# Regrouping TensorE's work in two attentions: two score steps together, values between two transpositions

## What is computed

```python
# "second attention" of the kernel: chunk_attention, 8 heads of 64, relative bias
s = einsum('bqhd,bkhd->bhqk', qch, kb) * scale + bias
p = softmax(where(valid, s, NEG_INF));   out = einsum('bhqk,bkhd->bqhd', p, vb)
# "third attention": mla_attention, 8 heads, q and k of 96 (64 + 32 rotated), v of 64
s = einsum('bqhd,bkhd->bhqk', qi, k) * scale
p = softmax(where(mask, s, NEG_INF));    out = einsum('bhqk,bkhd->bqhd', p, v)
```

## Time and profile before

| | |
|---|---|
| runs | 1180.93, 1180.98, 1180.99 us (median 1180.98) |
| profiled execution, its span | 1179.3 us |
| TensorE busy | 1169.2 us (99%) |
| VectorE, ScalarE, POOL busy | 571.2, 516.3, 455.4 us |
| second attention, first scores to last values | 661.3 to 706.5 us |
| third attention, first scores to last values | 726.2 to 775.1 us |

### The profile page before, as it was taken

One profiled execution on the slowest core, in us unless ns is written; L12 is line 12 of the kernel. 1 busy time (PEld: TensorE's weight loads), 2 busy tenths in 40 slices (PEclk: granted clock), 3 DMA queues, 4 the chain that ended last, 5 costly groups with the idle time before them and its releaser, 6 DMA issues.

```text
span 1179.3 us, 16136 instructions
## 1 busy us (share of the span) xinstructions
PE 1169.2 (99%) x5968; PEld 961.5 (82%) x5968; DVE 571.2 (48%) x1128; ACT 516.3 (44%) x816; POOL 455.4 (39%) x181
## 2 busy tenths in 40 slices
PE   9999999999999999999999999999999999999998
PEld 7887778988888888888988677789888888888887
DVE  4375245877777774212574567726434334340000
ACT  5444663634434442322546576835543443431110
POOL 6451224344344434444443211034434434434442
PEclk9999999999999999999999999999999999999999
DMA  8233122545544542223332110122322232212322
GB/s 310 81 108 107 37 76 104 205 176 190 213 184 174 211 156 83 98 98 109 127 137 91 54 37 1 37 72 73 107 108 94 84 107 107 75 70 98 98 98 96
DMA packets 27570, 132.39 MB, mean 112 GB/s; under 512 B 3456, under 2 KB 4608, under 8 KB 18688
## 3 DMA queue, kind: packets, MB, share of 16 engines
q1 hardware_dynamic: 25632, 129.23, 30.9%
q10 hardware_dynamic: 1888, 2.49, 0.7%
HBM read 129.61 MB, written 2.10 MB: 112 GB/s over the span
## 4 chain that ended last, share of the span: by engine, by line
PE 97%; ACT 2%; issue 0%; POOL 0%; DMA 0%; DVE 0%; DVEq 0%; ACTq 0%
PE psum L1544 87%; PE psum L1613 2%; PE psum L1625 2%; PE psum L2054 1%; PE psum L1774 1%; ACT prob L705 1%; PE psum L1867 1%; PE psum L1990 1%; ACT probT L688 1%; PE psum L1968 0%; POOL wl L488 0%; DMA gains_and_h<-x_first 0%; PE psum L1832 0%; PE psum L1998 0%; PE psum L1583 0%
## 5 line engine op out<-in xcount | busy, mean ns | idle before, releaser
L472 POOL TENSOR_TENSOR wl<-raw,wh 128x2048 fp32r<-128x2048 f32 (+2 forms) x89 | 365.6, 4108 | 495.1 <-ACT wh L621 285.3
L1544 PE MATMUL psum<-xh,wh 128*128 128x512 f32 (+1 forms) x1016 | 386.0, 380 | 1.2 <-POOL wl L488 1.1
L1544 PE MATMUL psum<-xl,wh 128*128 128x512 f32 (+1 forms) x1016 | 381.7, 376 | 0.0
L1544 PE MATMUL psum<-xh,wl 128*128 128x512 f32 (+1 forms) x1016 | 381.7, 376 | 0.0
L1190 DVE SCALAR_TENSOR_TENSOR scratch<-psum,cols,scratch 128x511 f32<-128x511 f32 (+1 forms) x176 | 131.7, 748 | 195.4 <-ACT scratch L766 186.4
L1544 PEld LDWEIGHTS psum<-xh,wh 128*128 128x128 f32 x1016 | 191.0, 188 | 40.6 <-issue 3.1
L1544 PEld LDWEIGHTS psum<-xh,wl 128*128 128x128 f32 x1016 | 191.1, 188 | 34.9
L1544 PEld LDWEIGHTS psum<-xl,wh 128*128 128x128 f32 x1016 | 191.2, 188 | 34.4 <-issue 0.2
L621 ACT ACTIVATE wh<-raw 128x2048 fp32r<-128x2048 f32 (+1 forms) x50 | 88.4, 1767 | 244.9 <-PE psum L1544 244.9
L1544 PE MATMUL psum<-acth,wh 128*128 128x512 f32 (+1 forms) x374 | 141.0, 377 | 0.0
L1544 PE MATMUL psum<-actl,wh 128*128 128x512 f32 (+1 forms) x374 | 140.8, 377 | 0.0
(11 more groups left out here) (264 smaller groups left out, 1383.1 us busy)
## 6 DMA issues: line engine op xcount, KB each, us to landing
raw<-stream SPq DMA_DIRECT2D x69, 1024.0 KB, 4.7
ada_raw<-ada SPq DMA_DIRECT2D x48, 512.0 KB, 5.4
raw<-down SPq DMA_DIRECT2D x32, 704.0 KB, 4.0
outT<-gains_and_h SPq DMA_DIRECT2D x8, 256.0 KB, 5.3
gains_and_h<-xT SPq DMA_DIRECT2D x7, 256.0 KB, 5.9
raw<-stream SPq DMA_DIRECT2D x7, 256.0 KB, 6.3
rel<-rel_tiles ACTq DMA_DIRECT2D x1, 1344.0 KB, 9.2
raw<-stream SPq DMA_DIRECT2D x2, 512.0 KB, 3.9
```

The costliest lines, as they stand in the source:

```text
L472: pool.tensor_tensor(wl[slot][:, 0:w], raw[slot][:, 0:w], wh[slot][:, 0:w].bitcast(F32), ALU.subtract).then_inc(lo_done, 1)
L1544: ins = pe.matmul(out, lhs[a], rhs[b], start=first and n == 0, stop=last and n == 2)
```

## The change

In the second and third attention TensorE's loop goes over pairs of steps, `u`: the scores of steps 2u and 2u+1, the transposition of step 2u-3, the values of steps 2u-5 and 2u-4, and the transposition of step 2u-2. Other work of the two steps (`beside`) stands behind both scores, but for u = 0. ScalarE keeps copy ahead of exponentials in even steps and takes the exponentials first in odd ones. The heads' high and low parts are taken one step later. The first attention keeps its order; its code is only moved into functions.

```diff
+        def values_of_pair(u):
+            last = STEPS // 2 + LAG // 2 - 1
+            return [x for x in (2 * u - 5, 2 * u - 4) if 0 <= x < STEPS] + ([STEPS - 1] if u == last else [])
+
+        def heads_step(a, p):
+            return TB * (p + 1) + LAG + (a > 0)
...
                 for step in range(STEPS + LAG):
-                    if TURN_LAG <= step < STEPS + TURN_LAG:
+                    turn = TURN_LAG <= step < STEPS + TURN_LAG
+                    behind = a > 0 and step % 2 == 1
+                    if turn and not behind:
                         turned(step)
...
+                    if turn and behind:
+                        turned(step)
                     if beside is not None:
                         beside(step)
-                    if step > TB + LAG - 1 and (step - LAG) % TB == 0:
-                        heads_high(a, (step - LAG) // TB - 1)
+                    for p in range(PAIRS - 1):
+                        if step == heads_step(a, p):
+                            heads_high(a, p)
...
+            def attend_by_two(a, ready, scores, v, prob, probT, ident, beside):
+                for u in range((STEPS + LAG) // 2):
+                    for step in (2 * u, 2 * u + 1):
+                        if step < STEPS:
+                            step_scores(a, step, ready, scores, None)
+                        if u == 0:
+                            beside(step)
+                    for step in (2 * u, 2 * u + 1):
+                        if u > 0:
+                            beside(step)
+                    if 0 <= 2 * u - TURN_LAG < STEPS:
+                        step_turned(a, 2 * u - TURN_LAG, prob, ident)
+                    for x in values_of_pair(u):
+                        step_values(a, x, v, probT)
+                    if 0 <= 2 * u + 1 - TURN_LAG < STEPS:
+                        step_turned(a, 2 * u + 1 - TURN_LAG, prob, ident)
...
-            attend(1, chunked_ready, chunked, None, v2, prob2, probT2, ident2, last_values_and_first_heads)
+            attend_by_two(1, chunked_ready, chunked, v2, prob2, probT2, ident2, last_values_and_first_heads)
...
-            attend(2, latent_ready, latent, None, v3, prob2, probT2, ident2, last_heads)
+            attend_by_two(2, latent_ready, latent, v3, prob2, probT2, ident2, last_heads)
```

More of the change, by code:

```diff
@@ L1257, in attend @@
                         dve.tensor_scalar(prob[V % 4][:, 1, 0:w], prob[V % 4][:, 1, 0:w], row_sum[:, c + 1:c + 2], None, ALU.mult).then_inc(att.norm, 1)
-                    if step > TB + LAG and (step - LAG - 1) % TB == 0:
-                        heads_low(a, (step - LAG - 1) // TB - 1)
+                    for p in range(PAIRS - 1):
+                        if step == heads_step(a, p) + 1:
+                            heads_low(a, p)
                     if after is not None and step >= STEPS:
@@ L1583, in norm_sum, with step_scores, step_turned, step_values @@
                 pe.matmul(SS_BANKS[j][:, half(j)], ones[:, :], ss_acc[:, half(j)], start=True, stop=True).then_inc(norm.ss, 1)
+            def step_scores(a, step, ready, scores, decays):
+                V, p, i, w = unit(a, step), step // TB, step % TB, width(step)
+                outs = scores_banks(a, V)
+                ready(step)
+                if a == 0 and step:
+                    pe.wait_ge(att.max, 2 * V - 1)
+                elif a == 1 and step >= 2:
+                    pe.wait_ge(att.max, 2 * V - 2)
+                elif step >= 2:
+                    pe.wait_ge(att.raw, 2 * step - 2)
+                for e in range(2):
+                    ins = scores(p, i, e, outs[e], w)
+                    if decays is None:
+                        ins.then_inc(att.qk, 1)
+                if decays is not None:
+                    for e in range(2):
+                        decays(p, e, outs[e], w).then_inc(att.qk, 1)
+            def step_turned(a, x, prob, ident):
+                V, i = unit(a, x), x % TB
+                pe.wait_ge(att.norm, 2 * V + 2)
+                if V >= 1:
+                    pe.wait_ge(att.ptc, V)
+                for e in range(2):
+                    for j in range(i + 1):
+                        ins = pe.transpose(TURN_BANKS[:, e, P * j:P * j + P], prob[V % 4][:, e, P * j:P * j + P], ident[:, :])
+                ins.then_inc(att.pt, 1)
+            def step_values(a, x, v, probT):
+                V, p, i = unit(a, x), x // TB, x % TB
+                pe.wait_ge(att.ptc, V + 1)
+                if a == 1 and x == 0:
+                    pe.wait_ge(att.max, 2 * unit(1, TB - 1) + 1)
+                if p >= 2 and i == 0:
+                    pe.wait_ge(heads.lo, PAIRS * a + p - 1)
+                for j in range(i + 1):
+                    for e in range(2):
+                        r, c = HD * e, HD * (2 * p + e)
+                        ins = pe.matmul(HEADS_BANKS[p % 2][r:r + HD, P * i:P * i + P], v[:, j, c:c + HD],
+                                        probT[V % len(probT)][:, e, P * j:P * j + P], start=j == 0, stop=j == i)
+                ins.then_inc(att.pv, 1)
             def attend(a, ready, scores, decays, v, prob, probT, ident, beside=None):
@@ L1587, in attend @@
                     if step < STEPS:
[L1588 to L1603, removed]
+                        step_scores(a, step, ready, scores, decays)
                     if beside is not None:
@@ L1606, in attend @@
                     if TURN_LAG <= step < STEPS + TURN_LAG:
[L1607 to L1613, removed]
@@ L1614, in attend @@
-                        ins.then_inc(att.pt, 1)
-                    for x in values_of(step):
[L1616 to L1627, removed]
+                        step_turned(a, step - TURN_LAG, prob, ident)
@@ new lines, in attend @@
+                    for x in values_of(step):
+                        step_values(a, x, v, probT)
[12 more added lines that the diff above has]
+                    for x in values_of_pair(u):
+                        step_values(a, x, v, probT)
+                    if 0 <= 2 * u + 1 - TURN_LAG < STEPS:
+                        step_turned(a, 2 * u + 1 - TURN_LAG, prob, ident)
```

## The result

| | before | after |
|---|---|---|
| median of four runs each | 1180.99 us | 1193.21 us |
| the runs | 1180.93 to 1183.23 | 1191.12, 1192.04, 1194.38, 1196.82 |
| profiled execution, its span | 1179.3 | 1189.4 |

The account below looks back on a forecast made before the run. TensorE bound the kernel, ScalarE a near second; changed, they would wait in turn. +4.0 (second attention) and +5.2 (third) make +9.2 on the 1179.3 span, 1188.5; the median lies 1.7 above, so 1190.2 us, range 1184.5 to 1192.5.

Parts of the forecast that it names:

- the cycle: Second and third attention: TensorE and ScalarE walk in turn over shared transposition banks, +0.8 and +2.0 us a period.
- half A: From the width-256 to the width-512 transposition: TensorE sets it, 4.32 us in the second attention, 5.57 in the third.
- half B: From the width-512 to the width-256 transposition: ScalarE sets it, 5.16 us in the second attention, 5.92 in the third.
- period: One head pair, four steps: 9.48 us for 8.68 in the second attention, 11.49 for 9.49 in the third.
- end of the second: Last values of the second attention end at 710.6 us where they ended at 706.55, +4.0.
- end of the third: The third attention ends at 780.35 us where it ended at 775.12, +5.2.
- joined scores: Score groups of widths 384 and 512 in a row: 1.70 us in the second attention, 3.10 in the third.
- waits for the copy: Sign: TensorE waits 1.4 to 1.8 us for ScalarE's copy before each width-256 transposition, none before width 512.
- Rivals 1 to 3: TensorE stays the bound, 1176.9 (5%); only one half long, 1187.0 (13%); that with hidden start and no 0.44 wait, 1184.2 (10%).
- the start: Start of the second attention: the last value products' copy delays step 3's exponential, from 670.89 to 671.94 us.
- the 0.4 wait: Third attention, between neighbouring exponential pairs: ScalarE waits for VectorE's scaled maximum, +0.44 us (between 0 and 0.54).
- rival 4: TensorE's clock falls to 1.2 GHz in the attentions' idle gaps: some 12 us more, 1202; chance 4%.

Follow-up runs that it names:

- experiment 1: The changed kernel with TensorE's new order kept, but ScalarE again copying ahead of the exponentials in every step: 1181.63 us, 1.0006 against the kernel before.
- experiment 2: The changed kernel with TensorE's old loop back and ScalarE's new order kept: 1188.52 us, 1.0066 against the kernel before.
- experiment 7: Changed kernel with unused products in TensorE's waits, second attention's last value half back ahead of step 3's scores: 1188.37 us; without the start's products, 1188.79.

## Why the prediction was right and where it failed

*The direction and the cycle*: right. It said a half from T(512) to T(256) is set by ScalarE and one from T(256) to T(512) by TensorE. In us, the trace's times less the 0.31 (second) and 3.87 (third) by which each stretch had begun late:

| | predicted | measured |
|---|---|---|
| half A, half B, second | 4.32, 5.16 | 4.31, 5.16 |
| half A, half B, third | 5.57, 5.92 | 5.52, 5.90 |
| period, second and third | 9.48, 11.49 | 9.47, 11.42 |
| T(1), T(3), T(5) of the second | 673.87, 678.07, 683.55 | 673.82, 677.97, 683.41 |
| end of the second | 710.6 (+4.0) | 710.18 (+3.56) |
| T(1), T(3) of the third | 737.66, 742.85 | 737.52, 742.62 |
| end of the third | 780.35 (+5.2) | 781.48, without 1.63 of clock 779.85 (+4.7) |

The joined scores took 1.70 and 3.01 (from 686.33 to 688.03, 754.89 to 757.90), for 1.70 and 3.10. The Trainium skill (TensorE: Matmul & The Clock Gate, "Part 3: Packing small matmuls"), read as the prediction did, gives no saving in the third; 0.10 against the separate 3.11 was saved. The waits for the copy are up to 1.93, 0.1 over the predicted 1.4 to 1.8. The sum of 9.2 is 1.0 above the 8.2 that the trace has without its fall: the second attention came out 0.4 and the third 0.5 below their terms, small things of one sign in every stretch.

*Rivals 1 to 3*: rightly low, as none came about. TensorE alone (experiment 1) neither paid nor lost; ScalarE's halves, the start and the 0.4 wait are all there.

*The step that failed* is rival 4, "TensorE's clock falls", at 4%, and the range drawn "not to 4": the sum has no term for the clock. The prediction had the gaps right (1.6 and 2.1 us of idle per period) and the rule that speaks of them, and then let "no row here shows one" count against it. The trace of before could not show one: its longest idle times on TensorE behind the start of the kernel are 1.28, in the first attention, and 1.12 some way ahead of it, shorter than the gaps that the change makes, and the clock is full at both:

```profile
153.76 0.85 PE L1613 MATMUL psum<-ident,prob 128*128 128x128 f32 x6 [1.28 <-ACT probT L688]
```

In all four runs of the changed kernel the mean clock was below 1. The size of the rival was wrong as well, 12 us where the clock cost 4.0 to 4.5 in the median: not every half A doubled, but one of them in the profiled run, at 1.63. By the spans the four runs lost 1.6 to some 7 us (1189.4 to 1195.1, against 1187.8, the profiled one without its fall). That is a term with a size and a spread, to be put in the sum, and not a rare other world. With it on a structural 1189.2 (1181.0 and 8.2) the range would have held the result; the forecast's 1190.2 came within 3.0 us only because a sum 1.0 too high stood in for a part of the clock, and that is luck.

What stays open: what decides whether a wait is followed by a fall. The falls in the profiled executions stand behind waits of 1.45 and 0.51, 1.47, 1.91 and 1.93; the same waits are followed by none in other executions, nor is the 2.01 of experiment 2. The Trainium skill (the same page, "HAM oscillation") ties the fall to idle gaps between groups of matmuls; filling the gaps fits that, but the waits of its example, 3 to 5 us, are longer than any here, and no run here tells what decides in a single case.

## What to carry to other kernels

When two engines share one buffer in turn, write down the cycle of each half (who starts whom, and what each has in hand meanwhile) before counting saved switches: putting two items of work ahead of the copy that frees the buffer cost some 8 us here (6.9 with the old order on TensorE), where the regrouping could have saved 4.1 at best. And where a change makes TensorE wait for 1 to 2 us at a time, put a clock term with a spread in the sum; a short row of unused products in the wait tells at once how much of a loss is the clock, and can take most of it back.

## What the runs showed of the hardware that was not expected

- The clock fell to 1.2 GHz behind waits of 1.45 to 1.93 us between dense stretches, in different places in different executions (five falls in four profiled ones), and came back by itself. A fall within the periods cost 1.6 us (1.57 to 1.63). It did not fall behind a wait of 2.01 in experiment 2, nor behind 1.28 in the kernel before.
- 5 and 8 small unused products in front of such waits did not lengthen the periods and gained 3.5 us; with the starts filled as well, 4.4. Where the wait was shorter than the products, in experiment 7, they hid 0.4 of a gain.
- With ScalarE's waits shortened in experiment 1, VectorE held TensorE in its place, and the second attention's period stayed within 0.1 us (8.74 for 8.68). With three engines at 7.9 to 8.3 of 8.7 us, none of the other orders tried won anything.
